# Expert weights of a two-layer diffusion block: transfers of 2 MB into eight slots, low parts in place, four slots for high parts

## The reference

```python
def _swiglu(h, wg, wu, wd):
    return (jax.nn.silu(h @ wg) * (h @ wu)) @ wd

def _moe(h, router, wg, wu, wd):
    logits = (h @ router).astype(jnp.float32)
    top_v, top_i = lax.top_k(logits, TOP_K)
    w = jax.nn.softmax(top_v, axis=-1)
    combine = jnp.sum(jax.nn.one_hot(top_i, N_EXPERTS, dtype=jnp.float32) * w[..., None], axis=-2)
    out = jnp.zeros_like(h)
    for e in range(N_EXPERTS):
        out = out + combine[..., e:e + 1].astype(h.dtype) * _swiglu(h, wg[e], wu[e], wd[e])
    return out
```

## Time and profile before

| | |
|---|---|
| median of three runs | 1901.88 us |
| profiled execution | 1900.44 us |
| its span, first to last instruction | 1898.7 us |
| mean granted TensorE clock | 0.982 |
| PE, DVE, ACT busy | 95%, 70%, 55% |
| expert weights | 336 transfers of 1024 KB, median 6.6 to 7.2 us from issue to landing |

### The profile page before, as it was taken

The page is one execution under the profiler, slowest core; times in us unless marked ns, Lnnn a source line. Parts: engine busy times, 40 slices in busy tenths (PEclk is TensorE's granted clock), DMA queues, the critical chain, the costliest instruction groups (busy, mean ns, idle before and its releaser), DMA issues.

```text
span 1898.7 us, 22616 instructions
## 1 busy us (share of the span) xinstructions
PE 1807.3 (95%) x8804; PEld 1463.1 (77%) x8804; DVE 1332.4 (70%) x1245; ACT 1046.4 (55%) x989; POOL 121.3 (6%) x128
## 2 busy tenths in 40 slices
PE   4999989999999999887999999999999999999997
PEld 2986578888888888566888787877878888888776
DVE  2478656333333367745888889888889898889888
ACT  3233744222222144554777677777777777767774
POOL 1020800000000012411000000000000000000000
PEclk9999989999999999997999999999999999999999
DMA  8325923532342124643999998999989999899995
GB/s 294 127 89 183 349 65 75 138 103 81 94 111 83 61 98 147 237 163 135 346 365 358 347 386 318 374 345 345 360 323 369 377 372 370 322 351 372 349 365 214
DMA packets 246198, 472.80 MB, mean 249 GB/s; under 512 B 10578, under 2 KB 60596, under 8 KB 246092
## 3 DMA queue, kind: packets, MB, share of 16 engines
q1 hardware_dynamic: 242000, 468.14, 69.4%
q10 hardware_dynamic: 4092, 3.20, 0.6%
HBM read 470.26 MB, written 1.05 MB: 248 GB/s over the span
## 4 chain that ended last, share of the span: by engine, by line
PE 58%; DMA 18%; DVE 14%; ACT 7%; issue 2%; POOL 1%; SPq 0%; ACTq 0%; POOLq 0%; DVEq 0%
PE bank L546 16%; PE bank L547 16%; PE bank L548 16%; DVE parts L1752 8%; DMA raw<-in_moe_w_up_dram 6%; DMA raw<-in_moe_w_down_dram 5%; DMA raw<-in_moe_w_gate_dram 5%; ACT parts L1439 5%; PE bank L564 2%; DMA raw<-in_ada_w_dram 2%; DVE parts L1737 1%; PE bank L793 1%; PE bank L1055 1%; PE bank L782 1%; PE bank L774 1%
## 5 line engine op out<-in xcount | busy, mean ns | idle before, releaser
L1752 DVE TENSOR_TENSOR parts<-raw,parts 128x2048 fp32r<-128x2048 f32 x336 | 765.7, 2288 | 107.6 <-ACT parts L1439 106.6
L1439 ACT ACTIVATE parts<-raw 128x2048 fp32r<-128x2048 f32 x336 | 643.7, 1919 | 252.2 <-DMA raw<-in_moe_w_up_dram 92.9
L546 PE MATMUL bank<-parts,XEr 128*128 128x512 f32 x896 | 356.7, 398 | 9.5 <-issue 4.1
L548 PE MATMUL bank<-parts,XEr 128*128 128x512 f32 x896 | 350.5, 391 | 0.0
L547 PE MATMUL bank<-parts,XEr 128*128 128x512 f32 x896 | 350.5, 391 | 0.0
L1300 ACT ACTIVATE parts<-raw 128x2048 fp32r<-128x2048 f32 (+1 forms) x62 | 113.2, 1831 | 271.1 <-PE bank L548 251.0
L1737 DVE TENSOR_TENSOR parts<-raw,parts 128x2048 fp32r<-128x2048 f32 (+1 forms) x62 | 135.7, 2193 | 137.6 <-ACT parts L1300 137.3
L546 PEld LDWEIGHTS bank<-parts,XEr 128*128 128x128 f32 x896 | 169.0, 189 | 50.4 <-issue 10.4
L548 PEld LDWEIGHTS bank<-parts,XEr 128*128 128x128 f32 x896 | 168.9, 189 | 36.0
L547 PEld LDWEIGHTS bank<-parts,XEr 128*128 128x128 f32 x896 | 169.2, 189 | 32.9
L546 PE MATMUL bank<-parts,HTr 128*128 128x512 f32 x448 | 176.1, 393 | 2.9 <-DVE parts L1752 2.4
(11 more groups left out here) (246 smaller groups left out, 2239.1 us busy)
## 6 DMA issues: line engine op xcount, KB each, us to landing
raw<-in_moe_w_gate_dram SPq DMA_DIRECT2D x112, 1024.0 KB, 6.7
raw<-in_moe_w_up_dram SPq DMA_DIRECT2D x112, 1024.0 KB, 7.2
raw<-in_moe_w_down_dram SPq DMA_DIRECT2D x112, 1024.0 KB, 6.6
raw<-in_ada_w_dram SPq DMA_DIRECT2D x28, 1024.0 KB, 8.0
more<-in_ada_w_dram SPq DMA_DIRECT2D x20, 1024.0 KB, 7.6
raw<-in_w_in_dram SPq DMA_DIRECT2D x12, 1024.0 KB, 5.1
raw<-in_ffn_w_gate_dram SPq DMA_DIRECT2D x22, 512.0 KB, 3.9
raw<-in_ffn_w_up_dram SPq DMA_DIRECT2D x22, 512.0 KB, 5.2
```

The lines of the kernel that those rows point to most:

```text
L546: nc.tensor.matmul(out, st[0], mv[0], start=start, stop=False)
L548: return nc.tensor.matmul(out, st[1], mv[0], start=False, stop=stop)
L1439: nc.scalar.activation(parts[:, n % PARTS, 0, :], raw[:, r, :], ACT.Copy).then_inc(hi_ready, 1)
L1752: return nc.vector.tensor_tensor(out, a, b, op)
```

## The change

A load now takes both halves of a gate, up or down item at once, 2 MB, into a pair of eight slots `loaded` (bytes 0 to 64 KB of a partition). The low part is written over the loaded value in the same slot (`low` is the same memory). The high parts have four slots of their own (`high`, 64 to 96 KB). SP waits no longer for low parts: the load of items m and m+1 waits until PE has used the items that lay in both slots before, the later of which is item m+1-8. ACT's split of item m waits, as before, for PE's use of item m-4. SP's loop over the pairs of experts is written out.

```diff
+WEIGHTS = 8
+LOAD = 2
...
+        loaded_t, = phase(("expert_loaded", WEIGHTS * 8 * KB, F32))
+        low_t, high_t = phase(("expert_low", WEIGHTS * 8 * KB, F32R), ("expert_high", PARTS * 8 * KB, F32R))
...
+        expert_loaded = [sem(f"expert_weights_loaded{i}") for i in range(WEIGHTS // LOAD)]
...
-        def parts_free(pair, n, part):
-
-            back = n < PARTS
-            kind, half, g = order[n - PARTS]
+        def used(m, part):
+
+            i, n = divmod(m, PAIR_ITEMS)
+            kind, half, g = order[n]
             extra = CREDIT if kind == "down" else 0
-            return used_sem[kind, half], pair * PAIR_SLICES + (part * PAIRS * PAIR_SLICES + g + 1 + extra
-                                                               - (PAIR_SLICES if back else 0))
+            return used_sem[kind, half], (part * PAIRS + i) * PAIR_SLICES + g + 1 + extra
...
-                        return [parts[:, n % PARTS, j, :].rearrange("p (k n) -> p k n", n=SLICE) for j in range(2)]
+                        m = i * PAIR_ITEMS + n
+                        return [w.rearrange("p (k n) -> p k n", n=SLICE) for w in (high[:, m % PARTS, :], low[:, m % WEIGHTS, :])]
...
-                with sp.Fori(0, PAIRS) as i:
-                    for n, (kind, half, g) in enumerate(order):
-                        e = i * 2 + g // EF_SLICES
-                        s = g % EF_SLICES
-                        sp.wait_ge(lo_ready, i * PAIR_ITEMS + (before + n - RAW + 1))
...
-                        sp.dma_start(dst, rows).then_inc(raw_loaded[n % RAW], 16)
+                for m in range(0, PAIRS * PAIR_ITEMS, LOAD):
+                    i, n = divmod(m, PAIR_ITEMS)
+                    kind, half, g = order[n]
+                    e, s = i * 2 + g // EF_SLICES, g % EF_SLICES
+                    free, count = used(m + LOAD - 1 - WEIGHTS, part)
+                    if count > 0:
+                        sp.wait_ge(free, count)
+                    if kind == "down":
+                        r0 = s * SLICE + half * 2 * P
+                        rows = io["moe_w_down"][0][e, r0:r0 + LOAD * 2 * P, :]
+                    else:
+                        r0 = half * 4 * P
+                        rows = io["moe_w_" + kind][0][e, r0:r0 + LOAD * 4 * P, s * SLICE:(s + 1) * SLICE]
+                    at = m % WEIGHTS
+                    dst = loaded[:, at:at + LOAD, :].rearrange("p s n -> p (s n)").rearrange("p (k n) -> p k n", n=rows.shape[1])
+                    sp.dma_start(dst, rows.rearrange("(k p) n -> p k n", p=P)).then_inc(expert_loaded[at // LOAD], 16)
...
-                r = n % RAW
-                act.wait_ge(raw_loaded[r], i * (16 * PAIR_ITEMS // RAW)
-                            + 16 * (loads_before[r] + part * PAIRS * PAIR_ITEMS // RAW + n // RAW + 1))
-                act.wait_ge(*parts_free(i, n, part))
-                nc.scalar.activation(parts[:, n % PARTS, 0, :], raw[:, r, :], ACT.Copy).then_inc(hi_ready, 1)
+                m = i * PAIR_ITEMS + n
+                at = m % WEIGHTS
+                act.wait_ge(expert_loaded[at // LOAD], 16 * (part * (PAIRS * PAIR_ITEMS // WEIGHTS) + m // WEIGHTS + 1))
+                free, count = used(m - PARTS, part)
+                if count > 0:
+                    act.wait_ge(free, count)
+                nc.scalar.activation(high[:, m % PARTS, :], loaded[:, at, :], ACT.Copy).then_inc(hi_ready, 1)
...
-                tt(parts[:, n % PARTS, 1, :], raw[:, n % RAW, :], parts_f[:, n % PARTS, 0, :], ALU.subtract).then_inc(lo_ready, 1)
+                m = i * PAIR_ITEMS + n
+                tt(low[:, m % WEIGHTS, :], loaded[:, m % WEIGHTS, :], high_f[:, m % PARTS, :], ALU.subtract).then_inc(lo_ready, 1)
```

More of the change, by code:

```diff
@@ L230, in build @@
         parts_f = parts_t[:, :].bitcast(F32).rearrange("p (s two n) -> p s two n", s=PARTS, two=2)
+        low = low_t[:, :].rearrange("p (s n) -> p s n", s=WEIGHTS)
+        loaded = loaded_t[:, :].rearrange("p (s n) -> p s n", s=WEIGHTS)
+        high = high_t[:, :].rearrange("p (s n) -> p s n", s=PARTS)
+        high_f = high_t[:, :].bitcast(F32).rearrange("p (s n) -> p s n", s=PARTS)
         row = [t[:, :] for t in row_t]
```

## The result

The changed kernel takes 1886.04 us (median of four runs, 1884.93 to 1890.20), the kernel before 1902.11 us (four runs, 1901.47 to 1907.29). The medians are 16 us apart, where 5.5 were forecast and the range ended at 1890.5. Rival 3 (all stops for weights go) had the right mechanism and was itself too small at 1890.4.

What follows compares the result with a forecast made beforehand. PE was taken to set the time, with weights arriving just in time. Weight stops (5.2 us) and HE waits (0.3) going made 5.5 us off 1901.88: forecast 1896.4 us, range 1890.5 to 1904.5.

Steps and rivals of the forecast that it cites:

- Rival 3: Experts' phase: all 10.7 us of weight stops and 0.8 us of HE waits go, 1890.4 us; chance 0.20.
- Between the two counts, 4.9 and 10.7, I take 7.8 us: PE's stop for weights today, between waits counted at the matmul (4.9) and at the weight load (10.7).
- A third stays: Of PE's 7.8 us stop for weights, two thirds (5.2 us) go; the rest stays because the margin is nil.
- Full queues nearly close the gap, with nothing over: Lean stretches' weight transfers would rise from 344 and 357 to 373 and 375 GB/s, just what PE eats.
- found DVE waiting 2.15 us for PE: Chain at 1061.19: DVE's wait and other work delayed the slot's refill to 8.5 us after landing, where 4.3 would do.
- 6.0 us of reserve: Old weight ring: a transfer can be 6.0 us late before PE stops, 4.2 in the split, 1.8 before it.
- any lateness of the landings goes into the next issue: Old release of weight transfers: a late landing delays the next issue for all 16 DMA engines.
- half the transfers: 168 weight transfers instead of 336: taken as 0 gain, the fixed part being hidden behind neighbouring transfers.
- the start: Before the first expert matmul at 897.31: items five to eight land some 15 us earlier, gain 0.
- the turns: Changes from one pair of experts to the next: PE's three stops, 4.1 us, stay.
- HE's waits: PE's transposes waiting for HE when DVE runs behind, 0.8 us: 0.3 us of it goes.
- Rival 1: Splits wait for the whole 2 MB pair to land: 4.8 us lost, 1906.7 us; chance 0.14.
- Rival 2: Memory gives 344 to 357 GB/s in lean stretches whatever is queued: no change, 1901.9 us; chance 0.20.

Runs made afterwards that it cites:

- e4: The changed kernel with 1 MB transfers released by PE, in six slots instead of eight: 1889.33 us.
- e6: The changed kernel with 1 MB transfers released by PE, in five slots instead of eight: 1897.82 us, one run.
- e7: The changed kernel with all its loads, but experts' splits and matmuls only for the first half of each item's contracted rows: 1806.84 us, one run.
- e10: The changed kernel with 1 MB transfers, each released by ACT's high part of the item four back: 1887.16 us.
- e11: The changed kernel with 1 MB transfers, old release by DVE's low part, only each item's first half split, all 12 matmuls kept: 1880.59 us.
- e1: The changed kernel with 1 MB transfers, each released by PE's use of the item eight back: 1887.37 us.
- e2: The changed kernel with 1 MB transfers and the old release by the low part of the item four back: 1902.39 us.
- e8: The changed kernel with 1 MB transfers, experts' splits and matmuls only for the first half of each item's contracted rows: 1805.89 us, one run.
- e5: The changed kernel with its 2 MB transfers released by PE, in six slots instead of eight: 1981.98 us, one run.

## Why the prediction was wrong

It had the place, and the mechanism in the main: the release by a late low part. Three steps of its sum failed, the first two by their size, and one row under the mechanism was misread.

1. *The size of today's stop: "Between the two counts, 4.9 and 10.7, I take 7.8 us".* The stop was 13.6 us, the waits for HE included, more than either count; the one at the weight load was called overstated and was still too small. PE's idle time is counted between a matmul's end and the next one's start, but a matmul lasts 0.39 us while its successor follows after 0.227. One stop of the kernel before, in the timeline of PE:

```profile
1262.91 0.39 PE L548 MATMUL bank<-parts,XEr 128*128 128x512 f32 x1
1263.68 0.50 PE L546 MATMUL bank<-parts,XEr 128*128 128x512 f32 x1 [0.38 <-DVE parts L1752]
```

The view says 0.38. The start is 0.77 after the last one instead of 0.227, so 0.54 late. The first matmul after a stop also takes longer before the next one starts, here 0.34 us where 0.23 is usual:

```profile
1081.81 0.50 PE L546 MATMUL bank<-parts,HTr 128*128 128x512 f32 x1 [0.55 <-DVE parts L1752]
1082.15 0.40 PE L547 MATMUL bank<-parts,HTr 128*128 128x512 f32 x1
1082.39 0.40 PE L548 MATMUL bank<-parts,HTr 128*128 128x512 f32 x1
```

Stops under 0.16 us don't show as idle time at all. Set side by side, matmul by matmul, the starts in the two traces differ by 13.8 us over the phase: 8.3 us at the 14 places where the kernel before shows idle time, 1.3 at the matmul behind each, 3.1 at 26 places that show none, and 1.0 spread thinly.

The rows on record had the true size: the earlier trace rows give 974 matmuls in 215 us without idle time, which is 272 in 60 us; 1260 to 1320 us has 256. The 16 missing are 3.6 us, where the busy time lacks 1.64. The four lean stretches together lack 7 + 16 + 5 + 23 = 51, 11.6 us, against 5.6 us of idle time. I read the column beside it.

2. *"A third stays".* None stayed. Two thirds of 13.6 us would have been 9.1; so of the 8.3 us between the forecast 5.5 and the 13.8 of the traces, about half is the size of the stop and half this third. With eight slots the first half can be 4.8 us late, of which 0.6 before ACT's split. ACT's longest wait for a landing is 2.1 us, and no stop of PE comes of it; e4, with 4.2 us, has no stops either. The working of these reserves held: 8.1 us for a landing against 7.8, and with 1.5 us (e6) the stops are back.

3. *"Full queues nearly close the gap, with nothing over",* on which the third rested. The 373 and 375 GB/s came from scaling the lean rates by the DMA share. The share is packets' time, and the packets of the lean stretch were themselves longer: 344 GB/s at 0.96, where e7 has 393 at 1.04, are 358 for a share of 1.00 against 378. With a full queue both grow, so the scaled rate was 5% too low. In e7 there was room of 4.9% over PE's need. In the changed kernel the queue needn't be full: its worst stretch has a share of 0.99.

The misread row is the "2.15 issue" at 1063.21 in the earlier trace rows: "found DVE waiting 2.15 us for PE". DVE was splitting then, as its timeline shows:

```profile
1063.14 2.30 DVE L1752 TENSOR_TENSOR parts<-raw,parts 128x2048 fp32r<-128x2048 f32 x1 [0.40 <-ACT parts L1439]
1065.35 0.68 DVE L1752 TENSOR_TENSOR HE<-bank,SGE 128x512 f32<-128x512 f32 x1
1065.95 1.40 DVE L2222 SCALAR_TENSOR_TENSOR ACC<-bank,top,ACC 128x512 f32<-128x512 f32 x2
```

The transfer issued at 1069.71 was released by the next item's low part. That item had landed at 1063.94, so its slot was refilled after 5.8 us, where 4.3 would do, and not after 8.5. DVE's order cost 1.5 us there, not the 4.2 with which rival 3 argued, and a wait for PE had no part in it.

*What made the old ring fail.* The prediction gave it 6.0 us of reserve on paper. With the measured landing of 6.9 us instead of 5.1 that is 4.2, as much as e4 has; yet e4 has no stops and the old ring had. The difference is that the old release comes behind the landing and both splits. Its loop has 6.9 of transfer, 1.93 and 2.30 of splits and 0.1 to the issue, 11.2 us for four items, just PE's 4 x 2.8. This sum alone proves little, since the 6.9 was measured inside the loop. But ACT stood waiting for the landing at 246 of 332 splits, so there was no slack to catch up what was once lost. In e10 and e11 the landing takes as long, the loop is 9.1 and 9.5 us, and ACT mostly waits for PE. The prediction wrote these numbers down one by one ("any lateness of the landings goes into the next issue") and never added them up. That the release is the cause is shown (e1, e2, e10); that it acts through the missing slack of the loop is the reading that fits all runs, and no single run isolates it.

The rest of the working stood: half the transfers gave 0 (e1, e8), the written-out order and the in-place low parts 0 (e2; the subtraction takes 2289 ns against 2288), the start 0 (897.50 against 897.31), the turns kept their 4.1 us. HE's waits, 0.8 us, went whole.

Rival 1 (the whole pair must land) is real with six slots (e5) and idle with eight. Rival 2 (no faster packets) is refuted by the changed kernel's own stretches at 364 to 373 GB/s and by e7. The rule of the Trainium skill quoted with it (DMA: Bandwidth & Descriptors, "Where 436 GB/s comes from", about 358 GB/s from HBM) does not hold for this core alone: 393 GB/s over 796 us in e7.

## What to carry to other kernels

Measure the stops of PE by counting matmuls in a stretch with stops and in one without, not by PE's idle time: here the count said 13.6 us and the idle time 5.9. Where a ring of slots passes through several engines, add its stages up and compare the sum with slots times pace; if they are equal, a late landing can't be made up. Here PE lost 13.6 us although every engine and the DMA had room, and releasing the slot by PE's own count brought them all back. Take the landing time for such a sum from the loop itself and look whether the stage behind it waits for it. Look at an engine's timeline before an "issue" in a chain of waits is called a wait. Before calling a transfer rate a limit, take PE's work out and see what the queue does when it is full.

## What the runs showed of the hardware

- A full queue gives 392 to 393 GB/s steadily, whether in pieces of 1 or 2 MB (e7, e8; splits and matmuls halved). At PE's demand of 374.5 GB/s the DMA share reads 0.97 to 1.00 as well (0.97 over 904 to 1864 us of the changed kernel), so a share near 1 didn't mean that the engines had no room.
- The first matmul after a stop of PE holds up the next one by some 0.11 us more than usual (0.34 against 0.23 at 1081.81 in the kernel before).
- 8.1 us for 2 MB (the changed kernel) and 5.4 to 5.5 us for 1 MB (e1) differ by 2.7 us, the time of 1 MB at 393 GB/s. Neither is the time of a lone transfer: with one of 1 MB issued every 2.8 us, about two are under way at a time.
